# Order of the two products inside a dense gate or up piece: all 512-column ones first, then all 256-column ones

## What is computed

```python
def swiglu(h, w_gate, w_up, w_down):
    return (jax.nn.silu(h @ w_gate) * (h @ w_up)) @ w_down

def first_block(x, ...):
    for l in range(DEPTH):
        x = x + token_mixer(rmsnorm(x, norm1_g[l]), ...)
        h = rmsnorm(x, norm2_g[l])
        if l % 2 == 0:
            x = x + swiglu(h, ffn_w_gate[j], ffn_w_up[j], ffn_w_down[j])
        else:
            x = x + moe_ffn(h, ...)
    return rmsnorm(x, final_g)

def second_block(x, ...):
    for l in range(DEPTH):
        x = x + 0.5 * swiglu_2(rms_norm(x, ffn1_norm[l]), ...)
        ...  # attention and convolution
        x = x + 0.5 * swiglu_2(rms_norm(x, ffn2_norm[l]), ...)
        x = rms_norm(x, post_norm[l])
    return x
```

## Time and profile before

| what | value |
|---|---|
| time, median of 3 runs | 2426.27 us (2425.06 to 2426.35) |
| span of the profiled execution | 2421.3 us |
| median less span | 5.0 us |
| TensorE matmul busy | 2383.2 us (98%), 12281 products |
| TensorE weight loads busy | 2008.5 us (83%) |
| VectorE busy | 1883.2 us (78%) |
| ScalarE busy | 1440.9 us (60%) |
| granted TensorE clock, mean | 0.995 of 2.4 GHz |

### The profile page before, as it was taken

The page is one execution under the profiler, slowest core; times in us unless marked ns, Lnnn a source line. Parts: engine busy times, 40 slices in busy tenths (PEclk is TensorE's granted clock), DMA queues, the critical chain, the costliest instruction groups (busy, mean ns, idle before and its releaser), DMA issues.

```text
span 2421.3 us, 33632 instructions
## 1 busy us (share of the span) xinstructions
PE 2383.2 (98%) x12281; PEld 2008.5 (83%) x12281; DVE 1883.2 (78%) x1913; ACT 1440.9 (60%) x1488; POOL 42.4 (2%) x66
## 2 busy tenths in 40 slices
PE   9999999999999999999999989999999999999998
PEld 8888897888888888888888878887888888878887
DVE  7766677889888888888888876669766766687765
ACT  5544455777777777777677754455644544556443
POOL 1000000000000000000000000020000000100000
PEclk9999999999999999999999999999999999999999
DMA  7555544999999899999999955543355555542552
GB/s 265 185 191 189 184 168 145 350 348 366 358 354 374 340 371 340 371 341 370 341 370 343 372 192 185 184 165 123 122 191 191 183 185 184 180 142 90 189 191 87
DMA packets 83240, 594.44 MB, mean 246 GB/s; under 512 B 9468, under 2 KB 9500, under 8 KB 11996
## 3 DMA queue, kind: packets, MB, share of 16 engines
q1 hardware_dynamic: 81216, 587.76, 67.2%
q0 software_dynamic: 1520, 4.40, 0.6%
q10 hardware_dynamic: 432, 1.31, 0.1%
HBM read 592.38 MB, written 1.05 MB: 245 GB/s over the span
## 4 chain that ended last, share of the span: by engine, by line
PE 92%; DVE 5%; ACT 1%; DMA 1%; issue 1%; DVEq 0%; SPq 0%; ACTq 0%
PE banks L1062 17%; PE banks L1115 9%; PE banks L1117 9%; PE banks L1121 9%; PE banks L1064 9%; PE banks L1140 8%; PE banks L1142 8%; PE banks L1141 8%; PE banks L1091 2%; PE banks L1376 2%; DVE lo L1680 1%; PE banks L1246 1%; PE banks L1161 1%; PE banks L1429 1%; PE banks L1406 1%
## 5 line engine op out<-in xcount | busy, mean ns | idle before, releaser
L1680 DVE TENSOR_TENSOR lo<-raw,hi 128x2048 fp32r<-128x2048 f32 x548 | 1253.9, 2290 | 218.6 <-ACT hi L564 214.7
L564 ACT CAST hi<-raw 128x2048 fp32r<-128x2048 f32 x550 | 1051.7, 1913 | 253.4 <-PE banks L1121 124.4
L1062 PE MATMUL banks<-xhl,hi 128*128 128x512 f32 x1776 | 629.5, 398 | 3.0 <-DVE gsum L1729 2.5
L1064 PE MATMUL banks<-xhl,lo 128*128 128x256 f32 x1776 | 498.3, 281 | 0.0
L1062 PEld LDWEIGHTS banks<-xhl,hi 128*128 128x128 f32 x1776 | 333.6, 188 | 86.6 <-DVE lo L1680 4.7
L1140 PE MATMUL banks<-hi,xhl 128*128 128x512 f32 x896 | 353.6, 395 | 1.1 <-issue 1.1
L1142 PE MATMUL banks<-hi,xhl 128*128 128x512 f32 x896 | 349.6, 390 | 0.0
L1141 PE MATMUL banks<-lo,xhl 128*128 128x512 f32 x896 | 348.9, 389 | 0.0
L1115 PE MATMUL banks<-hi,hh 128*128 128x512 f32 x872 | 342.9, 393 | 1.8 <-DVE hl L1700 1.8
L1117 PE MATMUL banks<-lo,hh 128*128 128x512 f32 x872 | 340.7, 391 | 0.0
L1064 PEld LDWEIGHTS banks<-xhl,lo 128*128 128x128 f32 x1776 | 335.3, 189 | 1.9
(11 more groups left out here) (362 smaller groups left out, 2498.9 us busy)
## 6 DMA issues: line engine op xcount, KB each, us to landing
raw<-in_moe_w_gate SPq DMA_DIRECT2D x112, 1024.0 KB, 4.9
raw<-in_moe_w_up SPq DMA_DIRECT2D x112, 1024.0 KB, 4.9
raw<-in_moe_w_down SPq DMA_DIRECT2D x112, 1024.0 KB, 4.9
raw<-in_ffn_w_gate SPq DMA_DIRECT2D x58, 1024.0 KB, 4.8
raw<-in_ffn_w_up SPq DMA_DIRECT2D x58, 1024.0 KB, 4.9
raw<-in_ffn_w_down SPq DMA_DIRECT2D x58, 1024.0 KB, 4.9
raw<-in_mix_pieces SPq DMA_DIRECT2D x46, 1024.0 KB, 4.9
raw<-in_mix_pieces SPq DMA_DIRECT2D x2, 768.0 KB, 4.5
```

The lines of the kernel that those rows point to most:

```text
L564: nc.scalar.copy(hi[:, hslot(S, c), 0:n], raw[:, c % RING, 0:n]).then_inc(S.hi_done, 1)
L1062: pe.matmul(bank[b + s][:, :], hi[:, hr, a:a + P], xhl[:, k, :], start=(k == 0), stop=False, skip_group_check=True)
L1064: mm = pe.matmul(bank[b + s][:, 0:T], lo[:, r, a:a + P], xhl[:, k, 0:T], start=False, stop=(k == KD - 1), skip_group_check=True)
L1680: v.tensor_tensor(lo[:, c % RING, 0:n], raw[:, c % RING, 0:n], hi[:, hslot(S, c), 0:n].bitcast(F32), ALU.subtract).then_inc(S.lo_done, 1)
```

## The change

In `pe_cols2` the inner loop over k is split. For the blocks of the call, first all `hi` products (512 columns) of both blocks are issued, then all `lo` products (256 columns). A piece of two blocks has sixteen of the one and then sixteen of the other, a call with one block eight and eight. Operands, banks, waits and the released semaphore are the same; the opening product of each bank (`start`) is still its first and the closing one (`stop`) its last.

```diff
@@ -1061,6 +1061,9 @@
                     a = k * FW + s * P
                     pe.matmul(bank[b + s][:, :], hi[:, hr, a:a + P], xhl[:, k, :], start=(k == 0), stop=False,
                               skip_group_check=True)
+            for s in blocks:
+                for k in range(KD):
+                    a = k * FW + s * P
                     mm = pe.matmul(bank[b + s][:, 0:T], lo[:, r, a:a + P], xhl[:, k, 0:T], start=False,
                                    stop=(k == KD - 1), skip_group_check=True)
             return mm
```

## The result

| | before | after |
|---|---|---|
| time, median | 2426.31 us (2425.06 to 2426.74) | 2412.93 us (2412.61 to 2416.74) |
| span of the profiled execution | 2421.3 us | 2411.4 us |
| a loop step of the dense stages | 16.79 us | 16.57 us |

The changed kernel takes 0.9947 of the time before, with a 95% interval of 0.9935 to 0.996: 13 us less by the medians, 10 to 16 by the interval, 9.9 by the spans of the two traces. The forecast was 2420.0 us, 6.3 us less. The direction was right and the gain larger.

What follows compares the result with a forecast made beforehand. Dense steps were taken as bound by TensorE's issue alone. Gaining 0.14 us in each of 48 loop steps and losing 0.04 in five first steps gave 6.3 us unrounded, so 2420.0 us; range 2413 to 2431, own range 2416 to 2422.

Steps and rivals of the forecast that it cites:

- What bounds the kernel: Dense steps: bound by TensorE's issue alone, busy all of 184.38 us in eleven steps, so each nanosecond gained moves the end.
- Undisturbed prices, 226.7 and 120 ns: Start-to-start times of 512- and 256-column products in settled rows; a pair sums to 346.7 ns against 353 in the loop.
- Borders from long to short at nothing: Inside a piece, going from 512- to 256-column products: cost 0, bounds -0.01 to 0 us.
- The toll of a seam, 0.06 us: Going from 256- to 512-column products, twice a step, at the up and down pieces: 0.06 us each time.
- The earlier trace: Ten 512-column products behind 128-column ones, from 539.41 us: 2.37 us against 2.27, read as a toll of 0.10 us.
- The five first steps, 0.2 us lost: First step of each dense stage, already at 11.11 us for 32 pairs: becomes 11.15, losing 0.04 us each.
- The first rival, no toll: The disturbed entry goes with the alternation: 0.26 us gained a step, 12.6 us in all, 2413.7 us; chance 0.17.
- The second and third rival: 234.3 ns products persist through up and down pieces (2429.9 us, chance 0.22), or into the gate piece too (2436.2 us, 0.08).
- The fourth rival: Order is nothing: the 6 ns a pair belong to the loop or buffers and stay; 2426.3 us, chance 0.09.
- Span to median: Median of the runs, 2426.27 us, lies 5.0 us above the profiled span of 2421.3; taken as untouched by the change.

Runs made afterwards that it cites:

- groups of four: Gate and up products issued as four long, then four short, in turn, against one for one in the kernel before: 0.999 (0.998 to 0.9999), loop step 16.69 us.
- groups of two: Gate and up products issued as two long, then two short, in turn, against one for one in the kernel before: 0.9962 (0.995 to 0.9975), loop step 16.59 us.

## Why the prediction was right, and where its size was off

- **What bounds the kernel**: right. What TensorE's issue gave up, 0.22 us a step, appears in the span, 9.9 us, and no wait took its place.
- **Undisturbed prices, 226.7 and 120 ns**: right. Gate's long products take 3.62 us for sixteen and its short ones 1.92; in the kernel with equal lengths, pure 512-column pieces with alternating buffers run at the same 226.7.
- **Borders from long to short at nothing**: right within its bounds (-0.01 to 0 us). In groups of four the short products take 0.47 us where 0.48 was due.
- **The toll of a seam, 0.06 us**: this is the term that was mis-sized. It came from today's down piece, the row with the closest operands, but that piece is entered from the slow alternation and not from settled short products. Measured: 3.65 less 3.62, 0.03 us, at the up piece. The down piece was left unchanged at 5.50 us in the sum and takes 5.47, so the same mistake counted there a second time. Together 0.03 + 0.03 us a step and the 0.02 us that the short products give back at their two borders: 0.08 us, which makes 0.14 into 0.22, and 6.3 into 10.5 us. The earlier trace rows was read too high as well: of the 0.10 us in the earlier trace rows, 0.06 are in the first product alone (539.41 to 539.70, 0.29 us), and the nine behind it lose 0.04.
- **The five first steps, 0.2 us lost**: the traces have 0.04 us, and not evenly. Their gate and up pieces lose 0.03 to 0.07 us in four stages. In the one that starts at 1437.08 us the kernel before was in the slow rhythm already (11.38 us), and the change gains 0.17.
- **The first rival, no toll**: 2413.7 us is closest to the time, but its mechanism is not what happened: the toll is halved, not gone. In the trace it would have made 12.6 us and a step of 16.53. The range reached down to 2413 for this rival's sake, and that the time is not clearly outside it is luck.
- **The second and third rival, a slow rhythm that holds on**: fell. The up piece's sixteen long products together lose 0.03 us, not 0.12.
- **The fourth rival, and with it one price for each length by itself, as the Trainium skill has it (TensorE: Matmul & The Clock Gate, "Back-to-back issue gap")**: fell, by 0.22 us a step. The trace differs in size as well: 226.7 and 120.0 ns where the formula gives 215.8 and 109.2.
- **Span to median**: the forecast took 5.0 us between the two as fixed. In the runs after, an execution takes 1.8 us more than its own span (2413.18 and 2411.4; 2415.34 and 2413.6). The rest, 3.2 us, was the distance of the profiled execution of before to the median of others, which does not carry over. Had the sum been made on the 1.8 us, it would be 2421.3 - 6.3 + 1.8 = 2416.8, and with the measured steps 2412.6.

What stays open is why products of two lengths disturb each other at all. The runs show that the price depends on the sequence and the entry (353, 349, 347 ns for the same pair), and speak against the weight buffer, the bank and waits. They don't exclude the weight loads or the recording, and they don't explain the slow rhythm of the earlier trace rows, which has one length only.

## What to carry to other kernels

Where a stream of products has nothing to wait for, read its price as the distance between starts over many instructions, for each length by itself and for the mix: a mix that costs more than the sum of its parts was put right here by order alone, at no cost in work or memory. Put products of one length in long rows, and turn every second piece round so that equal lengths meet; don't expect that moderate groups bring a moderate part of it, since groups of four kept half and groups of two nearly all. Take the toll of a new border from a row that is entered as the new one will be, not from the one with the same operands.

## What the runs showed of the hardware

- Weight load and product, back to back: 226.7 ns for 512 columns and 120.0 for 256, while the same two in turn take 353.
- One-for-one alternation of the two lengths has two rhythms, 347 and 353 ns a pair, both seen in one loop step.
- A seam from settled short to long products costs about 0.03 us, spent within the sixteen products behind it (3.65 us where 3.62 is undisturbed).
- The loss by alternation was there with one weight buffer (16.79 us a step) and with the other bank (11.29 us for the two pieces), and gone with equal lengths (19.95 us, the plain sum).
- Products of 512 columns alone can run slow too: 234.3 ns each in the mixer's output, before and after the change.
